# Decay matrices of the SSD heads: one broadcast matmul with Relu and Exp in place of five matmuls with an additive mask

## What is computed

```
ac[t]      = cumsum over t of dt[t, h] * a[h]              # a < 0, so ac falls with t
decay[t,s] = exp(ac[t] - ac[s])  for s <= t, 0 otherwise   # segsum, then exp
m[t,s]     = decay[t,s] * (C_t . B_s)                      # C.B is shared by the 8 heads of a group
y[t]       = sum over s of m[t,s] * (x[s] * dt[s])  + d[h] * x[t]
```

## Time and profile before

| | |
|---|---|
| median of 3 runs | 2356.21 us (2350.63 to 2359.89) |
| profiled execution, span | 2353.5 us; the page gives no other time for it |
| mean granted clock of PE | 0.971 of 2.4 GHz |
| the SSD heads, first decay matmul to the fourth LRU piece | 1419.13 to 1474.22 us |

### The profile page before, as it was taken

One profiled execution on the slowest core, in us unless ns is written; L12 is line 12 of the kernel. 1 busy time (PEld: TensorE's weight loads), 2 busy tenths in 40 slices (PEclk: granted clock), 3 DMA queues, 4 the chain that ended last, 5 costly groups with the idle time before them and its releaser, 6 DMA issues.

```text
span 2353.5 us, 33775 instructions
## 1 busy us (share of the span) xinstructions
PE 2226.4 (95%) x13726; PEld 1972.1 (84%) x13726; DVE 1707.6 (73%) x2136; ACT 1177.1 (50%) x1390; POOL 234.2 (10%) x183
## 2 busy tenths in 40 slices
PE   7899999998899999997999989899999999989998
PEld 7778888888678888887998987799989988868997
DVE  5667679994667679997776786787677776586555
ACT  3554356883644356874434764433343344534333
POOL 5200312212000302310000010000000020000000
PEclk9899999998999999998999999999999999999999
DMA  9129779994029779995884332488668743206651
GB/s 250 59 95 332 254 270 326 359 359 165 3 101 342 257 271 331 363 355 187 298 277 173 145 130 86 161 290 291 229 236 280 266 151 136 109 1 209 195 180 70
DMA packets 241451, 505.56 MB, mean 215 GB/s; under 512 B 10383, under 2 KB 104529, under 8 KB 241296
## 3 DMA queue, kind: packets, MB, share of 16 engines
q1 hardware_dynamic: 216144, 417.84, 50.7%
q10 hardware_dynamic: 21600, 77.09, 9.2%
q0 software_dynamic: 3552, 8.47, 1.5%
HBM read 502.31 MB, written 1.05 MB: 214 GB/s over the span
## 4 chain that ended last, share of the span: by engine, by line
PE 61%; DVE 9%; ACT 2%; issue 1%; DMA 0%; DVEq 0%; ACTq 0%
PE PS L1091 22%; PE PS L1107 10%; PE PS L926 7%; PE PS L1191 6%; PE PS L884 5%; PE PS L1290 2%; DVE WGL L2349 2%; PE PS L1310 2%; PE PS L1200 1%; PE PS L1354 1%; DVE AR L2352 1%; PE PS L1386 1%; PE PS L1570 1%; DVE XN L2349 1%; DVE AR L2349 1%
## 5 line engine op out<-in xcount | busy, mean ns | idle before, releaser
L2349 DVE TENSOR_TENSOR WGL<-ring,WGH 128x2048 fp32r<-128x2048 f32 (+1 forms) x291 | 599.8, 2069 | 226.2 <-ACT WGH L1778 116.9
L1091 PE MATMUL PS<-XTB,WGH 128*128 128x256 f32 x2816 | 516.3, 285 | 5.3 <-DVE XTB L2349 4.9
L1091 PEld LDWEIGHTS PS<-XTB,WGH 128*128 128x128 f32 x2816 | 447.5, 193 | 15.9 <-issue 8.1
L1091 PE MATMUL PS<-XTB,WGL 128*128 128x256 f32 x1408 | 400.0, 284 | 0.0
L1091 PEld LDWEIGHTS PS<-XTB,WGL 128*128 128x128 f32 x1408 | 271.6, 193 | 0.0
L2349 DVE TENSOR_TENSOR WDL<-ring,WDH 128x1024 fp32r<-128x1024 f32 (+1 forms) x136 | 216.9, 1595 | 32.3 <-ACT WDH L1945 22.9
L1945 ACT ACTIVATE WGH<-ring 128x2048 fp32r<-128x2048 f32 x96 | 183.4, 1914 | 102.6 <-PE PS L1191 39.6
L1778 ACT ACTIVATE WGH<-ring 128x1024 fp32r<-128x1024 f32 (+2 forms) x107 | 145.1, 1360 | 178.9 <-PE PS L926 61.1
L926 PE MATMUL PS<-XTB,WGH 128*128 128x256 f32 x1088 | 206.4, 291 | 12.6 <-DVE WGL L2349 9.8
L1988 ACT ACTIVATE XN<-PS 128x256 f32<-128x256 f32 x88 | 33.8, 384 | 352.4 <-PE PS L1091 326.8
L926 PEld LDWEIGHTS PS<-XTB,WGH 128*128 128x128 f32 x1088 | 173.2, 195 | 23.8 <-DVE WGL L2349 11.6
(11 more groups left out here) (522 smaller groups left out, 4450.6 us busy)
## 6 DMA issues: line engine op xcount, KB each, us to landing
FA<-in_ada_w ACTq DMA_DIRECT2D x144, 512.0 KB, 6.3
ring<-in_moe_w_up SPq DMA_DIRECT2D x64, 1024.0 KB, 7.0
ring<-in_moe_w_gate SPq DMA_DIRECT2D x64, 1024.0 KB, 7.9
ring<-in_moe_w_down SPq DMA_DIRECT2D x64, 1024.0 KB, 7.6
ring<-in_ffn_w_gate SPq DMA_DIRECT2D x44, 1024.0 KB, 5.8
ring<-in_ffn_w_up SPq DMA_DIRECT2D x44, 1024.0 KB, 10.3
ring<-in_ffn_w_down SPq DMA_DIRECT2D x44, 1024.0 KB, 7.4
ring<-in_hyb_w_in SPq DMA_DIRECT2D x10, 1152.0 KB, 6.6
```

Source lines behind the costliest of these rows:

```text
L1091: ins = mm(PS[:, 4 + b, m * T:(m + 1) * T], w_[:, b, w], x_[:, k, :], start=k == 0 and q == 0, stop=k == KD - 1 and q == 2)
L2349: return V.tensor_tensor(out_, x_, y_, op)
```

## The change

One matmul of 256 columns broadcasts row h of `AC` to all partitions; there is no mask. ACT then computes relu(ac[s] - ac[t]) in two instructions (256 and 128 columns, the second from columns 128 to 255 of the same bank) and takes exp of its negative over all 384 columns in place. Where s > t the difference is negative and becomes 0, so exp gives 1 there, and the triangle in `CBM` makes it 0. `EH` has four buffers instead of two and lies where the LRU's gate weights were. ACT's loop has 17 steps: Relu of head h, then Exp of head h - 1; `high` keeps its steps. A new semaphore `falls` counts the Relus; PE's `spread` waits for it where it waited for `eh`; `eh` counts one Exp a head. `ACD` is copied without a change of sign in one instruction instead of two. `mean_square(0)` moves from step 11 to step 10 on DVE, and `low` of n_proj+4 from step 14 to behind `gated(1)`.

```diff
--- before.py
+++ after.py
@@ -440,7 +440,7 @@
         AC = ROWB[:, 1, 0:T]
         DTR = ROWB[:, 1, T:2 * T]
         SPH = [GA[0:16, k, :] for k in range(4)] + [ROWB[0:16, 1, 2 * T:3 * T]]
-        EH = carve(11784, 2, MW)
+        EH = carve(9216 + 520, 4, MW)
         CBM = carve(11784 + 2 * MW, 2, MW)
         ACD = carve(11784 + 4096, 64)
         H2_RS = carve(11784 + 2048, 2, T)
@@ -1514,15 +1514,9 @@
                 def spread(h):
 
                     if h >= 2:
-                        pe.wait_ge(S("eh"), 2 * (h - 1))
-                    b = 4 + h % 2
-                    one = bc(ID[:, h:h + 1], (P, P))
-                    tri = CON[:, C_CAUS:C_CAUS + P]
-                    mm(PS[:, b, 0:P], tri, ID, start=True, stop=False)
-                    mm(PS[:, b, 0:P], one, AC[:, 0:P], start=False, stop=True)
-                    mm(PS[:, b, P:T], one, AC[:, P:T], start=True, stop=True)
-                    mm(PS[:, b, T:MW], tri, ID, start=True, stop=False)
-                    mm(PS[:, b, T:MW], one, AC[:, P:T], start=False, stop=True).then_inc(S("spread"), 1)
+                        pe.wait_ge(S("falls"), 2 * (h - 1))
+                    mm(PS[:, 4 + h % 2, 0:T], bc(ID[:, h:h + 1], (P, P)), AC, start=True, stop=True)\
+                        .then_inc(S("spread"), 1)
 
                 def head(h):
                     pe.wait_ge(S("mt"), h + 1)
@@ -1530,9 +1524,9 @@
                         pe.wait_ge(S("ys"), h // 2 - 1)
                     o = 64 * (h % 2)
                     b = 6 + (h // 2) % 2
-                    mm(PS[o:o + 64, b, 0:T], RG_XD[:, 0, 64 * h:64 * h + 64], EH[:, h % 2, 0:T],
+                    mm(PS[o:o + 64, b, 0:T], RG_XD[:, 0, 64 * h:64 * h + 64], EH[:, h % 4, 0:T],
                        start=True, stop=False)
-                    mm(PS[o:o + 64, b, P:T], RG_XD[:, 1, 64 * h:64 * h + 64], EH[:, h % 2, T:MW],
+                    mm(PS[o:o + 64, b, P:T], RG_XD[:, 1, 64 * h:64 * h + 64], EH[:, h % 4, T:MW],
                        start=False, stop=True).then_inc(S("head_ps"), 1)
 
                 def squares(g):
@@ -1548,7 +1542,7 @@
 
                 for h in range(18):
                     if h == 12:
-                        pe.wait_ge(S("eh"), 2 * 11)
+                        pe.wait_ge(S("falls"), 2 * 11)
                         squares(0)
                         lru_out(2)
                         pe.wait_ge(S("sq_out"), 1)
@@ -2232,13 +2226,18 @@
                     act.wait_ge(S("gelu_step"), 3 * q + 3)
                     f(H2[:, 2 * q:2 * q + 2, :], H2[:, 2 * q:2 * q + 2, :], ACT.Tanh, scale=0.7978845608028654)\
                         .then_inc(S("gelu_tanh"), 1)
-                for h in range(16):
-                    act.wait_ge(S("spread"), h + 1)
-                    if h >= 2:
-                        act.wait_ge(S("head_ps"), h - 1)
-                    for t, (c0, c1) in enumerate(((0, T), (T, MW))):
-                        f(EH[:, h % 2, c0:c1], PS[:, 4 + h % 2, c0:c1], ACT.Exp,
-                          bias=ACD[:, 16 * t + h:16 * t + h + 1]).then_inc(S("eh"), 1)
+                act.wait_ge(S("acd"), 1)
+                for h in range(17):
+                    if h < 16:
+                        act.wait_ge(S("spread"), h + 1)
+                        if h >= 4:
+                            act.wait_ge(S("head_ps"), h - 3)
+                        for t, (c0, c1) in enumerate(((0, T), (T, MW))):
+                            f(EH[:, h % 4, c0:c1], PS[:, 4 + h % 2, t * P:T], ACT.Relu, scale=-1.0,
+                              bias=ACD[:, 16 * t + h:16 * t + h + 1]).then_inc(S("falls"), 1)
+                    if h >= 1:
+                        act.wait_ge(S("falls"), 2 * h)
+                        f(EH[:, (h - 1) % 4, :], EH[:, (h - 1) % 4, :], ACT.Exp, scale=-1.0).then_inc(S("eh"), 1)
                     if h == 2:
                         high(r, r.n_proj + 1)
                     if h in (7, 10):
@@ -3061,8 +3060,7 @@
                     split_tiles(r.sb + KD // 2 + q, k, g)
 
                 dve.wait_ge(S("acd_ps"), 1)
-                c(ts(ACD[:, 0:32], PS[:, 1, 0:32], -1.0))
-                V.tensor_copy(ACD[:, 32:64], PS[:, 1, 32:64]).then_inc(S("acd"), 1)
+                V.tensor_copy(ACD, PS[:, 1, 0:64]).then_inc(S("acd"), 1)
                 dve.wait_ge(S("acd"), 1)
                 for t in range(TT):
                     for j in range(2):
@@ -3096,8 +3094,8 @@
 
                 for h in range(17):
                     if h < 16:
-                        dve.wait_ge(S("eh"), 2 * (h + 1))
-                        tt(EH[:, h % 2, :], EH[:, h % 2, :], CBM[:, h // 8, :]).then_inc(S("mt"), 1)
+                        dve.wait_ge(S("eh"), h + 1)
+                        tt(EH[:, h % 4, :], EH[:, h % 4, :], CBM[:, h // 8, :]).then_inc(S("mt"), 1)
                     if h in (2, 4, 6, 8):
                         gelu(h // 2 - 1)
                     if h in (1, 5):
@@ -3108,12 +3106,11 @@
                         ys((h - 3) // 2)
                     if h == 9:
                         gated(0)
-                    if h == 11:
+                    if h == 10:
                         mean_square(0)
-                    if h == 14:
-                        low(r, r.n_proj + 4)
                 ys(7)
                 gated(1)
+                low(r, r.n_proj + 4)
 
                 def normed(g):
                     inverse(H2_RS[:, g, :], H2_RS[:, g, :], "hyb", g)
```

## The result

Nine runs of the changed kernel have a median of 2365.17 us (2361.25 to 2369.41), nine of the kernel before 2355.92: +9.25 us, ratio 1.0036 with a 95% interval of 1.0026 to 1.0046. That is inside the forecast range of 2349 to 2367 and on the side that was forecast, but four times the forecast step of 2.2 us. The profiled execution has a span of 2366.6 us. It starts the heads at 1422.40 us, 3.3 later than the one before; over all profiles of this study that start lies anywhere between 1413.9 and 1422.6, also with code that is the same up to there, so I measure the stage from its own start.

The account below looks back on a forecast made before the run. It took PE (95% busy) as the bound, with DVE nearly as late and its tail ending the stage last; the walk's net +2.2 us on the 2356.21 median gave 2358.4 us, range 2349 to 2367.

Parts of the forecast that it names:

- the forecast step of 2.2 us: Third SSD output piece (n_proj+6) starts at 1496.8 instead of 1494.64, and all that follows shifts by the same 2.2 us.
- the forecast itself: Whole kernel: -2 to +6 us, 2354 to 2363 with the scatter of runs, chance 0.81.
- rival 2: PE's clock falls in the new holes: one fall before DVE's tail 2361, four 2370; two or more, chance 0.08.
- The walk: SSD heads in PE's time, stretch by stretch: +1.4, +0.2, +1.7, -2.8 us, then DVE's tail; n_proj+6 +2.2 us.
- The table: ScalarE's load for Exp runs after two Relus while PE waits: 1.28 us, bounds 0 and twice that.
- Exp of 384: New ScalarE Exp of 384 elements, SBUF to SBUF: 0.52 us, bounds 0.42 and 0.62.
- The saved matmuls: Decay matmuls on PE: 0.53 us against 1.21, 0.68 saved a head, 10.9 us over 16 heads.
- DVE's tail: VectorE from last `ys` to end of `low(6)`: 20.3 + 2.2 - 0.44 = 22.1 us, ending last.
- holes of 2 us and a little more can go either way: PE's granted clock may or may not fall behind such holes; no fall was put into the sum.
- the three holes that it put ahead of DVE's tail: PE idle before value matmul 0 (2.3 us), the squares (2.0) and value matmul 14 (2.0).
- The first (bound by PE): Head loop stays bound by PE: decay's 10.9 us and the 3.14 hole go, up to 14 us, 2342; chance 0.09.
- The third: Relu and Exp need different ScalarE tables: 32 loads, 41 us less some 8, about 2390; chance 0.02.

Follow-up runs that it names:

- the kernel with filled holes: Changed kernel with dummy matmuls on TensorE in six holes, those before value matmul 6 no longer waiting for a skip term: 2359.77 us, ratio 1.0013 to before.
- the early remainder: Exp behind its own Relu, plus a one-element Exp ahead of the loop and VectorE's first remainder ahead of product 0: 2350.57 us, ratio 0.9974 to before.
- the second profile: The changed kernel run again unaltered, in a later group on the same chip: 2362.43 us, ratio 1.0022 to before, stage 92.5 us.
- the first with dummies: Changed kernel with dummy matmuls in six holes, those before value matmul 6 waiting for a skip term: 2363.1 us, ratio 1.0034 to before.
- the last version: Exp behind its own Relu, early table load and first remainder, group 0's norm at step 11, ScalarE's n_proj+4 copy one step later: 2347.29 us, ratio 0.9958.

## Why the prediction was right, and where it was too small

- **How far the range was luck.** The range held the time by its width. 2365.17 lies outside the 2354 to 2363 of the forecast itself, to which 0.81 was given; it is inside 2349 to 2367 because that range took in three falls of the clock. What happened is rival 2, to which 0.08 was given; at its price of 2.8 a fall, three of them on 2358.4 make 2366.8 (in the stage they cost 5.6 us together, not 8.4).
- **The walk.** All five stretches came out with the clock at full: the marks of the kernel with filled holes are 12.27, 24.14, 38.03, 55.18 and 77.27 for 12.08, 24.06, 37.89, 55.55 and 77.7. The forecast of +2.2 us for the order of the queues measured +1.8 there (88.5 for 86.7).
- **The table** stands where it was put, between Relu 1 and Exp 0, at 1.28 us; Exp followed 0.01 after it. The 2.66 that the Trainium skill (ScalarE: Activation LUTs, "What ACT_TABLE_LOAD costs") gives for a switch does not show here, and the row was the better guide. Exp of 384 took 0.52, the middle of its bounds. The load's share of the time wasn't measured by itself, only with the early remainder: 2.2 us of the stage for both, in the kernel with Exp behind its own Relu.
- **The saved matmuls.** A head of decay and value takes PE 1.42 us as computed (0.68 less), visible in the run with Exp behind its own Relu.
- **DVE's tail.** 21.9 us for the 22.1 computed. That moving one remainder is neutral holds in the stage of both kernels.
- **What was too small: the clock.** The step that failed is the choice to put no fall into the sum ("holes of 2 us and a little more can go either way") and to leave two or more of them a chance of 0.08. Its own rows had a fall behind the shorter hole (2.33 us at 1400.33) and none behind 2.39; at even odds, the three holes that it put ahead of DVE's tail (2.3, 2.0 and 2.0) would bring two falls or more in half of the cases. In the first profile three falls came ahead of the last head: behind value 0, in LRU piece 1, and in the squares and LRU piece 2. The table's columns, changed less holes filled, price them at 0.7, 1.7 and 3.2 us, on either side of the 2.8 that I took from the old kernel. With the 1.8 of the walk they make the 7.4 us by which n_proj+6 starts later (in the second profile 4.1 and 1.8 for 5.8). The fourth, behind value 14, slows value matmuls 14 and 15 (1.93 us up to LRU piece 3, 1.26 with the holes filled; the difference is in the 3.2) and is hidden by DVE's tail from there on. The fall in LRU piece 1 stands behind a hole of 1.57 us, which I hadn't counted as a danger at all: I looked at the longest holes of the stage, and not at several in a row.
- **The rivals.** The first (bound by PE) needed an order that this change doesn't have; given that order it came true in part: heads at 1.32 to 1.42 us and LRU piece 3 6.2 us earlier than before (48.92 for 55.09), not the 14 of the rival, since holes of 1.80, 0.85, 1.33 and 2.11 us and two falls were left. The second is what happened, with three falls for its two or more. The third is excluded: 32 Relus and 16 Exps alternate with one load.
- **What stays open.** The total moved by 9.3 in the first timing and 5.7 in the second; the stage explains 7.4 and 5.8 of the profiled executions, whose spans lie 13.1 and 2.5 above the one before (2366.6 and 2356.0 for 2353.5). The rest lies outside it: ahead of the stage the changed kernel took 1422.40 us in one profile and 1413.87 in the other. I can't say what sets that, nor what of the difference between the two timings is chance.

## What to carry to other kernels

Splitting an operation in two on an in-order engine and lagging its second half by one step looks like pipelining, but it makes each result wait for the next item's input, and it costs most where other work stands between two items. Before moving work off the busiest engine, walk the queue of the engine that feeds it, item by item, with all that is queued between; here that gave the order's cost to half a microsecond. And price a schedule with many short waits on TensorE twice: once for the waits, once for the clock.

## What the hardware showed

The granted clock fell behind holes that were shorter than the old kernel's 3.14 us: after one of 2.42 us, after one of 1.80 (before value matmul 0 with Exp behind its own Relu; 0.50 from 1428 to 1430), and in the stretch behind one of 0.40 and one of 1.57 (0.57 from 1447 to 1451). The length of a hole alone did not decide it. Before the first SSD output piece it fell behind 1.88 us in two kernels (0.57 from 1484 to 1488 with the remainder moved in the old one, 0.60 from 1488 to 1492 in the first with dummies) and stayed at 1.00 behind 1.87 in a third (the second with dummies). It also stayed at 1.00 where the longest hole in the heads was 0.9 (holes filled, the same kernel) and 1.33 (the last version). Filling a hole with matmuls whose result nobody reads was enough to hold it, and delayed nothing where they ended before the wait did.
